# Up weights of the Strassen products: from SyncE's queue to GpSimd's, in a one-core encoder block

## The reference: what is computed

```python
h = _layernorm(ALPHA * h + mix, ln1_g[l], ln1_b[l])
ff = (jax.nn.silu(h @ w_ffn_gate[l]) * (h @ w_ffn_up[l])) @ w_ffn_down[l]
h = _layernorm(ALPHA * h + ff, ln2_g[l], ln2_b[l])
```

## Time and profile before

| | |
|---|---|
| median of 3 runs | 1723.31 us (1721.21 to 1724.41) |
| the profiled execution | 1720.79 us, its span 1719.1 us |
| PE busy | 1711.2 us, 100% of the span |
| DVE busy | 1185.5 us, 69% |
| ACT busy | 831.1 us, 48% |
| POOL busy | 95.0 us, 6% |
| granted clock of TensorE | 1.000 |

### The profile page before, as it was taken

How to read it: one execution, slowest core, us unless ns; L and a number is a source line. 1 busy time by engine, 2 the same in 40 slices (tenths; PEclk the granted TensorE clock), 3 DMA queues, 4 the chain that set the end, 5 groups by cost and what they waited for, 6 DMA issues and landing times.

```text
span 1719.1 us, 20700 instructions
## 1 busy us (share of the span) xinstructions
PE 1711.2 (100%) x8868; PEld 1432.6 (83%) x8868; DVE 1185.5 (69%) x998; ACT 831.1 (48%) x680; POOL 95.0 (6%) x87
## 2 busy tenths in 40 slices
PE   9999999999999999999999999999999999999999
PEld 8888888898888888888888888888888888888886
DVE  5765655668675846444666779888989898865445
ACT  5455544454544445444444626455545545554332
POOL 0000002212131300000000000000000000000000
PEclk9999999999999999999999999999999999999999
DMA  9766655445444556756787948787887886878553
GB/s 345 249 253 208 210 193 196 172 166 187 166 161 172 187 192 225 269 180 229 254 272 230 409 166 270 230 256 216 270 255 240 245 248 163 268 244 306 196 196 122
DMA packets 121334, 387.44 MB, mean 225 GB/s; under 512 B 8608, under 2 KB 43808, under 8 KB 102688
## 3 DMA queue, kind: packets, MB, share of 16 engines
q1 hardware_dynamic: 112384, 364.56, 62.1%
q0 software_dynamic: 2720, 10.49, 3.3%
q10 hardware_dynamic: 6144, 11.14, 1.7%
HBM read 359.82 MB, written 25.69 MB: 224 GB/s over the span
## 4 chain that ended last, share of the span: by engine, by line
PE 97%; DVE 1%; DMA 1%; ACT 0%; SPq 0%; issue 0%; DVEq 0%; ACTq 0%
PE pair L1992 17%; PE pair L1994 17%; PE pair L1993 17%; PE pair L1966 9%; PE pair L1964 5%; PE pair L2272 4%; PE pair L2273 4%; PE pair L2271 4%; PE side L2252 3%; PE side L2253 3%; PE side L2251 3%; PE pair L2252 1%; PE pair L2253 1%; PE pair L2251 1%; DMA raw<-in_stream 1%; PE pair L1976 1%
## 5 line engine op out<-in xcount | busy, mean ns | idle before, releaser
L1277 DVE TENSOR_TENSOR weight_lo<-raw,weight_hi 128x2048 fp32r<-128x2048 f32 x210 | 482.2, 2298 | 361.4 <-ACT weight_hi L892 360.0
L892 ACT ACTIVATE weight_hi<-raw 128x2048 fp32r<-128x2048 f32 x210 | 402.4, 1916 | 523.1 <-DMA raw<-in_stream 522.9
L1992 PE MATMUL pair<-weight_hi,act_both 128*128 128x512 f32 x672 | 267.9, 399 | 0.9 <-DVE weight_lo L1277 0.9
L1994 PE MATMUL pair<-weight_hi,act_both 128*128 128x512 f32 x672 | 262.2, 390 | 0.0
L1993 PE MATMUL pair<-weight_lo,act_both 128*128 128x512 f32 x672 | 261.9, 390 | 0.0
L1966 PE MATMUL pair<-act_both,weight_hi 128*128 128x512 f32 x600 | 211.2, 395 | 0.0
L1176 ACT ACTIVATE part_hi<-part_raw 128x2048 fp32r<-128x2048 f32 x60 | 113.8, 1913 | 125.4 <-DVE part_raw L1746 51.1
L1964 PE MATMUL pair<-act_both,weight_lo 128*128 128x256 f32 x640 | 173.0, 280 | 0.0
L1726 DVE TENSOR_TENSOR part_lo<-part_raw,part_hi 128x2048 fp32r<-128x2048 f32 x60 | 136.8, 2287 | 40.5 <-ACT part_hi L1176 40.4
L1992 PEld LDWEIGHTS pair<-weight_hi,act_both 128*128 128x128 f32 x672 | 126.3, 188 | 27.4 <-issue 1.9
L1994 PEld LDWEIGHTS pair<-weight_hi,act_both 128*128 128x128 f32 x672 | 126.2, 188 | 26.7
(11 more groups left out here) (308 smaller groups left out, 2763.5 us busy)
## 6 DMA issues: line engine op xcount, KB each, us to landing
raw<-in_stream SPq DMA_DIRECT2D x256, 1024.0 KB, 5.1
part_raw<-in_stream SPq DMA_DIRECT2D x30, 1024.0 KB, 7.2
scratch<-spill ACTq DMA_DIRECT2D x40, 256.0 KB, 3.7
part_raw<-in_stream POOLq DMA_DIRECT2D x10, 1024.0 KB, 10.8
ln_rows<-in_ln_rows SPq DMA_DIRECT2D x6, 1024.0 KB, 9.1
gate<-scratch SPq DMA_DIRECT2D x12, 512.0 KB, 6.8
ff_scratch<-ff_blocks SPq DMA_DIRECT2D x11, 512.0 KB, 4.4
ff_land<-ff_scratch SPq DMA_DIRECT2D x44, 128.0 KB, 5.3
```

The lines of the kernel that those rows point to most:

```text
L892: act.activation(hi_of(n), raw_of(n), ACT.Copy).then_inc(extra_h if extra(n) else h_ready, 1)
L1277: dve.tensor_tensor(lo_of(n), raw_of(n), hi_of(n).bitcast(F32), ALU.subtract)\
L1992: pe.matmul(out, hi[:, k0 + k, tok], w_hi[:, k, :], start=first and k == 0, stop=False)
L1994: mm = pe.matmul(out, lo[:, k0 + k, tok], w_hi[:, k, :], start=False, stop=last and k == 3)
```

## The change

The 40 loads of up weights (`load_part`, 1 MB each: 5 ahead of the loop, 3 in each of five blocks, 5 more in each of the first four) leave SP's program and are put into POOL's, with the same waits as before (only the wait for `h_done` ahead of the first W_A is written out again). POOL's ten adding transfers stay on POOL, and stand now between these loads, in one order. SP keeps the plain pieces, the down pieces and the turned rows (`save_ff`, `fetch_ff`).

```diff
@@ SP
-            load_part(0, 0, W_B)
-            load_part(0, 0, W_E)
             loads(first + 4, first + 4 + AHEAD)
...
-            load_part(0, 0, W_A)
             loads(first + 7, first + 8)
...
-            sp.wait_ge(piece_used, first + 8)
-            load_part(0, 0, W_G0)
-            load_part(0, 1, W_G1)
             for p in range(BLOCKS):
-                done = PRODUCTS * p
-                sp.wait_ge(part_used, done + 1)
-                load_part(p, 1, W_A)
                 load_plain(p, 3)
-                sp.wait_ge(part_used, done + 3)
-                load_part(p, 1, W_B)
                 load_plain(p, 4)
-                sp.wait_ge(part_used, done + 4)
-                load_part(p, 1, W_E)
...
-                sp.wait_ge(part_used, done + 13)
-                load_part(p + 1, 1, W_G1)
-                load_plain(p + 1, 2)
+                for k in range(3):
+                    load_plain(p + 1, k)
@@ POOL
-            for p in range(BLOCKS):
-                for s in range(2):
-                    pool.wait_ge(part_sum, 3 * (2 * p + s) + 1)
-                    pool.dma_start(part_of(W_B).rearrange("p (h c) -> p h c", h=2),
-                                   up[2 * p + 2][:, :, s * half:(s + 1) * half], accum_op=ALU.add).then_inc(third_sum, 16)
+            def sum_t3(p, s):
+
+                pool.wait_ge(part_sum, 3 * (2 * p + s) + 1)
+                pool.dma_start(part_of(W_B).rearrange("p (h c) -> p h c", h=2), up_part(2 * p + 2, 2 + s), accum_op=ALU.add)\
+                    .then_inc(third_sum, 16)
+
+            pool.wait_ge(piece_used, FIRST["ffn"])
+            load_part(0, 0, W_B)
+            load_part(0, 0, W_E)
+            pool.wait_ge(h_done, 16)
+            load_part(0, 0, W_A)
+            pool.wait_ge(piece_used, FIRST["ffn"] + 8)
+            load_part(0, 0, W_G0)
+            load_part(0, 1, W_G1)
+            for p in range(BLOCKS):
+                done = PRODUCTS * p
+                sum_t3(p, 0)
+                pool.wait_ge(part_used, done + 1)
+                load_part(p, 1, W_A)
+                pool.wait_ge(part_used, done + 3)
+                load_part(p, 1, W_B)
+                pool.wait_ge(part_used, done + 4)
+                load_part(p, 1, W_E)
+                sum_t3(p, 1)
+                if p == BLOCKS - 1:
+                    break
+                pool.wait_ge(part_used, done + 7)
+                load_part(p + 1, 0, W_A)
+                pool.wait_ge(part_used, done + 9)
+                load_part(p + 1, 0, W_B)
+                pool.wait_ge(part_used, done + 10)
+                load_part(p + 1, 0, W_E)
+                pool.wait_ge(part_used, done + 12)
+                load_part(p + 1, 0, W_G0)
+                pool.wait_ge(part_used, done + 13)
+                load_part(p + 1, 1, W_G1)
```

More of the change, by code:

```diff
@@ L698, in ffn_part @@
                 return src[:, :, q % 2 * half:(q % 2 + 1) * half]
[L700 to L704, removed]
             def load_plain(p, j):
@@ L775, in _ @@
                     break
-                sp.wait_ge(part_used, done + 7)
-                load_part(p + 1, 0, W_A)
                 load_plain(p, 7)
[L779 to L786, removed]
-                sp.wait_ge(part_used, done + 13)
-                load_part(p + 1, 1, W_G1)
-                load_plain(p + 1, 2)
+                for k in range(3):
+                    load_plain(p + 1, k)
             load_plain(BLOCKS - 1, 7)
@@ L868, in _ @@
             half = 4 * 256
-            up = stream[FIRST["ffn"]:FIRST["ffn"] + dict(PHASES)["ffn"]]\
-                .rearrange("(c h m f) p e -> m f c p h e", h=2, m=2, f=2)[1, 1]
-            for p in range(BLOCKS):
-                for s in range(2):
-                    pool.wait_ge(part_sum, 3 * (2 * p + s) + 1)
-                    pool.dma_start(part_of(W_B).rearrange("p (h c) -> p h c", h=2),
-                                   up[2 * p + 2][:, :, s * half:(s + 1) * half], accum_op=ALU.add).then_inc(third_sum, 16)
+            ffn = stream[FIRST["ffn"]:FIRST["ffn"] + dict(PHASES)["ffn"]].rearrange("(c h m f) p e -> m f c p h e", h=2, m=2, f=2)
@@ new lines, in up_part, with load_part @@
+            def up_part(column, q):
+                return ffn[1, q // 2][column][:, :, q % 2 * half:(q % 2 + 1) * half]
+            def load_part(p, s, w):
+                c0 = 2 * p + 1
+                column, q = {W_A: (c0, s), W_B: (c0 + 1, s), W_E: (c0 + 1, 2 + s), W_G0: (c0, 2), W_G1: (c0, 3)}[w]
+                pool.dma_start(part_of(w).rearrange("p (h c) -> p h c", h=2), up_part(column, q)).then_inc(part_in[w], 16)
+            def sum_t3(p, s):
+                pool.wait_ge(part_sum, 3 * (2 * p + s) + 1)
+                pool.dma_start(part_of(W_B).rearrange("p (h c) -> p h c", h=2), up_part(2 * p + 2, 2 + s), accum_op=ALU.add)\
+                    .then_inc(third_sum, 16)
```

## The result

The changed kernel takes 1734.53 us in the median of four runs (1733.93 to 1736.78), the kernel before 1723.07 (1721.21 to 1724.41): a ratio of 1.0070, with a 95% interval of 1.0059 to 1.0082, and so 11.5 us more. The profiled execution took 1733.93 us.

The account below looks back on a forecast made before the run. PE was taken to bound the kernel; 9.4 us idle, 0.6 at j3, 1.3 slow restart and 0.5 in later blocks make 11.8, on 1723.3 giving 1735.1 us. Its own range was 1731 to 1739, with 80% between 1729 and 1742.

Parts of the forecast that it names:

- The bound: Whole kernel: PE bounds it, so moving transfers gains at most about 1 us, while lateness beyond a piece's room costs time.
- SP's side: SP's queue: dropping forty issues of 0.37 to 0.56 us and their waits is worth 0, at most 1 us.
- The first adding transfer: Block 0: issued at about 1065.1 us behind two loads, landing at 1078.5, making PE late at j2.
- a rival: POOL's queue: held by its own transfers, each issue waits and most pieces are late; above 1745 us, 4%.
- 9.4 us: PE at j2 of block 0: idle time from starting at 1082.8 instead of 1073.37 us; bounds 5.9 and 11.6.
- The lower bound: First adding transfer: the shortest seen issue to landing, 9.9 us, puts the landing at 1075.0 and PE's idle at 5.9.
- The restart: PE behind the gap in block 0: 1.3 us for a slow restart, above 0.6 for DVE's low half of j3.
- The later blocks: Blocks 1 to 4: adding transfers land 1 to 2 us later, just hidden; 0.5 us in all, bounds 0 and 6.
- The sum: Whole kernel: 9.4 + 0.6 + 1.3 + 0.5 = 11.8 us, giving 1735.1 us, 0.7% slower.

Follow-up runs that it names:

- E1: Changed kernel with only block 0's first adding transfer moved ahead of POOL's wait for column 0 and of W_G0 and W_G1; 1722.52 us, ratio 0.9995.
- E3: Changed kernel built with dynamic_dma_scratch_size 1792 instead of 1024; 1733.83 us, ratio 1.0057.
- E7: Changed kernel with block 0's first adding transfer right behind the wait for column 0, ahead of W_G0 and W_G1; 1728.78 us, ratio 1.0033.
- E2: Changed kernel with W_G0 and W_G1 of all blocks back on SP, POOL keeping the wait for column 0; 1733.35 us, ratio 1.0057.
- E8: Changed kernel with 40 matmuls, results thrown away, put on PE just ahead of j2 of block 0; 1734.52 us, ratio 1.0068.
- E4: Changed kernel with block 0's W_G1 put behind the first adding transfer, leaving the wait and W_G0 ahead; 1731.88 us, ratio 1.0041.
- E5: E1 with each later block's first adding transfer also waiting for the last product of the block before; 1722.61 us, ratio 1.0000.

## Why the prediction was right

**The bound.** It holds. PE does the same 8868 matmuls, and what the late piece cost it is the loss: 10.5 us idle and 1.88 behind the gap are 12.4 of the 12.54 us by which the five blocks grew. SP's side was worth 0, as said: E1 has all loads on POOL and equals the kernel before.

**The first adding transfer.** The place (j2 of block 0), the single gap, and the chain from the transfer over ACT and DVE to PE are as forecast. Of the two numbers behind it one was far off and one near. The issue was forecast 1065.1 - 1062.5 = 2.6 us after the blocks' start and came 8.1 after it. Two things were wrong in it: an ordinary load costs POOL 0.72 us, not the 1.21 taken from the adding transfer, and POOL was held for 6.1 us, which I had given 4% as a rival. It is what that rival says, but for one adding transfer of ten, the only one that came while two loads were under way. In block 2, for one, W_G0 was issued at 1223.10 and landed in 5.9 us, before the adding transfer's turn at 1232.58. The landing was forecast at 16.0 us and measured at 17.16. It survived the wrong issue because it was worked out from the transfers' work and not from the issue: without the pause, in E3, it was 15.90. So the mis-sized term is the **9.4 us** of idle PE, measured as 10.5, and the step that made it so is "the adding transfer at 1062.7 + 2 x 1.21", which reckoned with no hold of POOL.

The lower bound, 9.9 us from issue to landing, was the right figure for a transfer with no load ahead of it: E7's took 1076.24 - 1067.01 = 9.2 us. With two loads under way at its issue it was never within reach (14.2 us in E2, 14.0 in E3). The changed kernel's own took 9.0 us, since it was issued only when W_G0 had landed.

**Queue or work.** A load behind the adding transfer on the same queue did it no harm: in E7 W_G0, issued 0.76 us behind it, landed 11.0 us after its issue, and didn't keep the adding transfer from landing in 9.2. And that the loads ahead stand in the same queue made no difference of its own. In E2 they are in SP's queue, the adding transfer was issued 1.27 us earlier than in E3 (0.62 against 1.89 us after the start) and landed 1.09 earlier: 14.2 and 14.0 us from issue to landing. What counted in these runs is the work issued ahead, in whichever queue.

**The restart.** 0.6 + 1.3 = 1.9 us were forecast, 1.88 measured, but that they meet is luck. The 1.3 stood midway between no slow restart and one of 3 us in place of the 0.6; no run shows either number. What came is nine matmuls about 0.43 us apart instead of 0.227: 1.88 us and not 3, with no wait for DVE at j3. That wait is real, 0.51 us in E8, but the slow matmuls hide it, so that without them only 0.94 of the 1.88 us would come back. The granted clock, 1.00 in the blocks before the change, reads 0.50 from 1079 us on, with PE idle since 1074.1, and 0.50 still under the nine matmuls.

**The later blocks.** 0.5 us forecast, 0 measured. The room at j2 of block 1 went from 2.05 us to 1.79 us: the subtraction ends at 1166.33, PE comes at 1168.12.

```profile
1164.04 2.29 DVE L1737 TENSOR_TENSOR part_lo<-part_raw,part_hi 128x2048 fp32r<-128x2048 f32 x1 [1.98 <-ACT part_hi L1187]
```

```profile
1168.12 0.39 PE L2262 MATMUL side<-part_hi,form_hi 128*128 128x512 f32 x1
```

So W_G1 just ahead of it costs about 0.3 us of room there. Seen from the block's start, ACT could begin on W_B 0.4 us later than before the change in blocks 1 and 4, 0.9 in block 2 and 1.2 in block 3, where 1 to 2 had been forecast for all. The room hid it each time, and W_G1 had been in flight beside the transfer before the change too.

**The sum.** In the trace 10.5 + 1.88 + 0 against 9.4 + 1.9 + 0.5. The errors of +1.1 and -0.5 partly cancelled, which is luck of about half a microsecond. These terms add up to 12.4 us, where the medians differ by 11.5; that the forecast of 1735.1 lies within 0.6 us of the median owes another microsecond to scatter between executions.

## What to carry to other kernels

Before a transfer is put into another engine's program, list what stands ahead of it there, waits first: here one urgent transfer behind a wait that has nothing to do with it made the five blocks 5.1 us longer (E7), with two loads and the pause behind that wait too 12.5, and the dearer issues of 40 loads nothing (E1). Size such a delay by the work that the DMA engines must do up to its landing, not by its time of issue: in E3 that was 6.2 us earlier than in the changed kernel, and the landing 1.3. And where PE is the bound, count a gap longer than it is: in the profiled executions gaps of 3.2 to 10.5 us were followed by 9 to 14 matmuls at about half pace, 1.7 to 2.9 us. A longer gap didn't cost more there: 1.7 us behind 3.2 (E7), 2.9 behind 5.9 (E4), 1.9 behind 10.5. The granted clock fell 6.5 us before PE restarted in the changed kernel, 0.8 us before in E4, and 0.2 us after in E7.

## What was not expected of the hardware

- With `dynamic_dma_scratch_size=1024`, POOL's queue had three 1 MB loads under way (E1), but not an adding transfer and two loads. The issue that would have made it so held POOL until the oldest transfer had landed (6.09 us here, 4.71 in E4, 7.54 in E7), and with 1792 four went out from 1065.38 to 1068.21 us without a pause (E3). The profile shows it as an idle time released by "issue". SP's queue showed no such hold: before the change it issued three loads from 1062.68 to 1065.40, and the first to land took 8.6 us.
- POOL issues an ordinary load in 0.72 us in the median (1.23 for the one right behind the adding transfer in E7) and an adding transfer of the same size in 1.23, SP a load in 0.37 to 0.56.
- A gap of 3.2 us was followed by a slow restart (E7's profile: nine matmuls 0.36 to 0.43 us apart, the granted clock at 0.50 from 1082 to 1084 us).
- E5's adding transfers, issued 1.4 us later, landed 0.9 to 2.1 us earlier than E1's. No run settles why.
